# The last stage's norm as a factor per token, and the experts' sums in another place

## The chip, the core and the metric

The kernel runs on one core of one Trainium2 chip. The metric is the time of one execution on the device, in microseconds (us), the median of a few runs. The kernel before took 3516.21 us, median of 3 runs (3515.45 to 3517.61).

## The reference, cut to what matters

The model is two blocks one after the other on 512 tokens of width 1024. What the change touches is the very end: the mixture of experts of the second block, its residual add, and the final norm.

```python
def expert_choice_ffn(h, w_router, w_gate, w_up, w_down):
    ...
    top_aff, top_idx = lax.top_k(jnp.swapaxes(aff, 1, 2), cap)
    xe = jax.vmap(lambda hb, ib: hb[ib])(h, top_idx)
    hid = jax.nn.silu(jnp.einsum('becd,edf->becf', xe, w_gate)) * jnp.einsum('becd,edf->becf', xe, w_up)
    ye = jnp.einsum('becf,efd->becd', hid, w_down) * top_aff[..., None].astype(h.dtype)
    combine = lambda ib, yb: jnp.zeros((L, D), yb.dtype).at[ib.reshape(-1)].add(yb.reshape(-1, D))
    return jax.vmap(combine)(top_idx, ye)
...
        x = x + g2 * expert_choice_ffn(h, w_router[l], w_gate[l], w_up[l], w_down[l])
    return rmsnorm(x, norm_f)
```

There are 16 experts with 64 tokens each. Every expert has a gate, an up and a down matrix of 1024 x 1024 in f32, so the three matrices of all experts are 192 pieces of 1 MB (64 each for `eg`, `eu` and `ed`). The final `rmsnorm` divides each token by the root of its mean square over the 1024 features and multiplies feature by feature with `norm_f`.

## The kernel before

Each stage of the program is a class with one method per engine (`pe`, `act`, `dve`, `pool`, `sp`). The order of the work on an engine is the order in which these methods issue it, stage after stage, written out by hand. Engines meet at semaphores: `P.tick(key)`, `S.tick(key)`, `V.tick(key)` count finished work of TensorE, ScalarE and VectorE, and `e.wait_ge(P.at(key))` waits for it.

The activations stand feature by token: `k.xT[:, c, :]` is chunk c of 8 (128 features x 512 tokens). Two stages matter here.

**Experts.** The experts are taken in 8 pairs (`pr`). For a pair, TensorE runs six wide products (`wide_pe`): m = 0 to 3 are the two halves of the gate and up products, m = 4 and 5 the two halves (512 features each) of the down product. Each is done in two steps `kh`, and each step (16 matmuls of 512 columns) needs two weight pieces of 1 MB. SyncE issues the 24 pieces of a pair into a ring of 11 slots; a slot is loaded again when TensorE has finished the step that read it. In the loop of a pair TensorE does, in this order: m = 0 to 3; the sums of the pair before (`y_pe(pr - 1)`); the transposes of the hidden layer (`hidT`, banks 6 and 7); the gathered tokens of the next pair (`xT_pe`); m = 4 and 5. ScalarE and VectorE then turn banks 4 and 5 into a high and a low part `yhi`, `ylo` (ticks `ye`, one for each half), scaled by the router's weight.

The sums `y` scatter the pair's 128 rows back to the 512 tokens: for each of the 8 chunks c, two matmuls with a one-hot matrix into bank 4 + c % 4, and on VectorE (`y_dve`) one `stt` (line 175) that adds bank times gain into `k.xT[:, c, :]`. For chunk c of 4 or more TensorE waits until VectorE has read chunk c - 4. On VectorE the eight adds stand after the two halves of silu and `hid` (lines 175 and 165) and ahead of the copy of `hidT` (line 2749). The sums of the last pair come after its down product. There VectorE also adds up squares: `stat_act` squares chunk c on ScalarE into one of two buffers, `stat_dve` adds the square into `nacc`, and it stands directly behind the `stt` of the same chunk.

**Output.** One matmul with a matrix of ones adds `nacc` over the partitions and spreads the sum (128 x 512). VectorE makes the mean (line 171) and the reciprocal (line 441), ScalarE the root, all on 128 x 512. VectorE multiplies the eight chunks of x with the norm's weight and this factor (line 175), TensorE turns them back to token by feature with 32 transposes of 128 x 128 (line 282) into six banks, VectorE and ScalarE copy the banks out, and ScalarE issues four DMAs of 128 tokens (512 KB each) to `out_x` (line 2814).

Of the kernel before, what the change touches and what calls it, by code (L numbers as in the profile page):

```python
# [13 lines left out]
D = 1024  # L14
# [2486 lines left out]
class Experts(Dense):  # L2501
# [3 lines left out]
    def __init__(self, k, m):  # L2505
# [22 lines left out]
        self.hid = [piece(4), piece(5)]  # L2528
        self.hidT = [v3(piece(6), 8), v3(piece(7), 8)]
# [3 lines left out]
        self.ends = [(self.V, ("add", 7)), (self.P, ("y", 7, 7))]  # L2533
# [19 lines left out]
    def wide_pe(self, e, pr, m, bank, src):  # L2553

        for kh in range(2):
# [27 lines left out]
    def y_pe(self, e, pr):  # L2583
        k, P, S, V = self.k, self.P, self.S, self.V
        e.wait_ge(V.at(("ye", pr, 1)), V.at(("oh", pr)))
        for c in range(8):
            if c >= 4:
                e.wait_ge(V.at(("y", pr, c - 4)))
            elif c >= 2 and pr < 7:
                e.wait_ge((S if c == 3 else V).at(("xT", pr + 1, c - 2)))  # L2590
            b, cs = k.bank[4 + c % 4], slice(c * 128, c * 128 + 128)
            mm(e, b[:, :], self.yhi[:, cs], self.oh[pr % 2], True, False)
            mm(e, b[:, :], self.ylo[:, cs], self.oh[pr % 2], False, True).then_inc(*P.tick(("y", pr, c)))

    def pe(self, e):
# [18 lines left out]
        for pr in range(8):  # L2614
# [6 lines left out]
            if pr:  # L2621
                self.y_pe(e, pr - 1)
# [10 lines left out]
            for h in range(2):  # L2633
                self.wide_pe(e, pr, 4 + h, B[4 + h], self.hidT[x])
        self.y_pe(e, 7)
# [6 lines left out]
    def act(self, e):  # L2642
# [39 lines left out]
        for c in range(8):  # L2682
            self.stat_act(e, c, k.xT[:, c, :], V.at(("y", 7, c)))
# [10 lines left out]
    def y_dve(self, e, pr):  # L2694
        k = self.k
        for c in range(8):
            e.wait_ge(self.P.at(("y", pr, c)))
            y = k.xT[:, c, :]
            stt(e, y, k.bank[4 + c % 4][:, :], k.MOD[:, 40 + c, 0:1], y, ALU.mult, ALU.add).then_inc(*self.V.tick(("y", pr, c)))
            if pr == 7:  # L2700
                self.stat_dve(e, c, y)

    def dve(self, e):
# [53 lines left out]
        self.y_dve(e, 7)  # L2757
# [18 lines left out]
class Output(Dense):  # L2776


    def __init__(self, k):
        super().__init__(k, "out", "out")  # L2780
        k.reset()
        self.ot = [k.al(1024) for _ in range(4)]
        self.dma = [k.count(f"out_x{i}") for i in range(4)]

# [4 lines left out]

    def pe(self, e):  # L2790
        k, P, S, V, B = self.k, self.P, self.S, self.V, self.k.bank
        self.enter(e)
        self.norm_pe(e, B[7], 512, self.before.V.at(("add", 7)))
        for m in range(8):
            i, k0 = m // 2, 4 * (m % 2)
            if m >= 6:
                e.wait_ge((S if m % 2 else V).at(("ot", m - 6)))
            for c in range(4):
                e.wait_ge(V.at(("scaled", k0 + c)))
                p = k.tr(e, B[m % 6][:, c * 128:c * 128 + 128], k.hT[:, k0 + c, i * 128:i * 128 + 128])  # L2800
            p.then_inc(*P.tick(("ot", m)))
        yield

    def act(self, e):
        k, P, S, V, B = self.k, self.P, self.S, self.V, self.k.bank
        r = k.rstd
        self.enter(e)
        e.wait_ge(V.at("recip"))
        act(e, r, r, ACT.Sqrt).then_inc(*S.tick("rstd"))
        for i in range(4):  # L2810
            e.wait_ge(P.at(("ot", 2 * i + 1)))
            e.h.copy(self.ot[i][:, 512:1024], B[(2 * i + 1) % 6][:, :]).then_inc(*S.tick(("ot", 2 * i + 1)))
            e.wait_ge(V.at(("ot", 2 * i)), S.at(("ot", 2 * i + 1)))
# [3 lines left out]
    def dve(self, e):  # L2817
        k, P, S, V, B = self.k, self.P, self.S, self.V, self.k.bank
        self.enter(e)
        self.norm_dve(e, B[7], 512)  # L2820
        e.wait_ge(S.at("rstd"))
        for c in range(8):
            stt(e, k.hT[:, c, :], k.xT[:, c, :], k.col("normf", c), k.rstd, ALU.mult, ALU.mult).then_inc(
                *V.tick(("scaled", c)))
        for i in range(4):
            e.wait_ge(P.at(("ot", 2 * i)))
            e.h.tensor_copy(self.ot[i][:, 0:512], B[(2 * i) % 6][:, :]).then_inc(*V.tick(("ot", 2 * i)))
# [155 lines left out]
```

## Time and profile before

| what | value |
| --- | --- |
| median of 3 runs | 3516.21 us |
| the profiled execution's own time | 3518.45 us |
| span of its profile | 3516.6 us |
| TensorE busy, share of the span | 3132.0 us, 89% |
| VectorE busy | 1820.3 us, 52% |
| ScalarE busy | 1090.3 us, 31% |
| mean granted TensorE clock | 0.93 of full speed |
| HBM traffic over the whole span | 125 GB/s |

The span runs from the first to the last event of the profile; the execution's own time is 1.85 us longer. Busy times are shares over very different stages. The experts run from about 3001 us to 3494 us of the span, and in most of that the DMA engines move 421 GB/s; from 3469 us on they are idle until the output leaves. The granted clock is either 1.00 (2.4 GHz) or 0.50 (1.2 GHz) in any short stretch, and a mean of both in a longer one.

### The profile page before, as it was taken

How to read it: one execution, taken by the hardware profiler on the slowest of the kernel's cores; microseconds unless marked ns; L12 is line 12 of the kernel's file. 1: busy time of each engine (PE TensorE's matmuls, PEld its weight loads, DVE VectorE, ACT ScalarE, POOL GpSimd, SP SyncE). 2: the span in 40 equal slices, each digit the busy share in tenths (PEclk: the TensorE clock that was granted, in tenths of full speed). 3: DMA queues.
4: the chain of work that ended last, by engine and by line, in shares of the span. 5: the costliest groups of instructions: out<-in, count | busy, mean ns of one | idle time of the engine just before them, and what ended most of it. 6: DMA issues, size and time to landing. Idle time of an engine off the chain costs nothing.

```text
span 3516.6 us, 40774 instructions
## 1 busy us (share of the span) xinstructions
PE 3132.0 (89%) x16694; PEld 2358.2 (67%) x16694; DVE 1820.3 (52%) x3294; ACT 1090.3 (31%) x2156; POOL 41.2 (1%) x75
## 2 busy tenths in 40 slices
PE   7999998879999999999898789999778976788786
PEld 6777667767878878888677678887566974232332
DVE  5444546676656565454566764445763676121213
ACT  3222234353333243332343542222443542000001
POOL 0000000000000000000000000000000100000000
PEclk9999988879999999999898789999788888899998
DMA  4544411102223222221211012222011012899994
GB/s 176 182 168 156 144 48 42 43 25 86 94 72 120 86 94 90 74 77 61 83 48 48 25 60 97 95 96 99 36 60 61 2 62 95 342 421 421 421 421 207
DMA packets 68162, 443.25 MB, mean 126 GB/s; under 512 B 9604, under 2 KB 9732, under 8 KB 21640
## 3 DMA queue, kind: packets, MB, share of 16 engines
q1 hardware_dynamic: 61056, 423.65, 31.7%
q10 hardware_dynamic: 5224, 10.44, 0.8%
q0 software_dynamic: 1696, 6.55, 0.5%
q8 instruction: 132, 2.16, 0.3%
q14 instruction: 54, 0.44, 0.0%
HBM read 435.10 MB, written 5.51 MB: 125 GB/s over the span
## 4 chain that ended last, share of the span: by engine, by line
PE 68%; DVE 17%; DMA 8%; ACT 6%; issue 1%; ACTq 0%; DVEq 0%; POOLq 0%
PE ps L155 66%; DMA b<-in_eu 8%; DVE b L175 7%; DVE b L165 5%; ACT b L181 3%; PE ps L282 1%; DVE b L170 1%; ACT b L382 1%; ACT b L180 1%; DVE b L171 1%; DVE b L721 1%; DVE b L441 1%; ACT L181 0%; DVE b L1813 0%; DMA b<-in_xt 0%
## 5 line engine op out<-in xcount | busy, mean ns | idle before, releaser
L155 PE MATMUL ps<-b,b 128*128 128x512 f32 (+8 forms) x13952 | 2893.2, 399 | 280.9 <-DVE b L165 120.3
L155 PEld LDWEIGHTS ps<-b,b 128*128 128x128 f32 (+4 forms) x13952 | 2159.8, 188 | 986.0 <-issue 342.0
L165 DVE TENSOR_TENSOR b<-b,b 128x1024 fp32r<-128x1024 f32 (+6 forms) x852 | 704.2, 832 | 334.4 <-ACT b L382 230.4
L382 ACT CAST b<-b 128x1024 fp32r<-128x1024 f32 (+2 forms) x408 | 390.9, 960 | 441.0 <-PE ps L155 436.0
L165 DVE TENSOR_TENSOR b<-ps,b 128x64 f32<-128x64 f32 (+4 forms) x601 | 207.7, 356 | 260.8 <-PE ps L155 223.9
L181 ACT ACTIVATE b<-b 128x512 f32<-128x512 f32 (+6 forms) x303 | 170.5, 567 | 316.6 <-DVE b L175 163.4
L175 DVE SCALAR_TENSOR_TENSOR b<-ps,b 128x512 f32<-128x512 f32 (+3 forms) x296 | 150.5, 529 | 217.0 <-PE ps L155 190.1
L165 DVE TENSOR_TENSOR b<-b,ps 128x512 f32<-128x512 f32 (+1 forms) x106 | 71.8, 678 | 291.6 <-PE ps L155 291.1
L175 DVE SCALAR_TENSOR_TENSOR b<-b,b,b 128x512 f32<-128x512 f32 (+4 forms) x292 | 181.1, 641 | 68.4 <-ACT b L181 62.9
L155 PE MATMUL ps<-b 64*64 64x64 f32 (+8 forms) x2272 | 190.1, 278 | 16.4 <-DVE b L1994 9.2
L155 PEld LDWEIGHTS ps<-b 64*64 64x64 f32 (+3 forms) x2272 | 146.2, 150 | 52.1 <-issue 25.9
L1379 ACT CAST b<-b 128x512 fp32r<-128x512 f32 x88 | 54.6, 620 | 399.8 <-DVE b L165 399.8
L282 PE MATMUL ps<-b,b 128*128 128x128 f32 (+2 forms) x470 | 84.3, 320 | 83.4 <-DVE b L175 32.7
L175 DVE SCALAR_TENSOR_TENSOR b<-ps,b,b 128x512 f32<-128x512 f32 (+2 forms) x144 | 80.6, 589 | 130.5 <-ACT b L181 112.4
L282 PEld LDWEIGHTS ps<-b,b 128*128 128x128 f32 (+2 forms) x470 | 62.0, 163 | 116.1 <-DVE b L175 42.0
L181 ACT ACTIVATE b<-b,b 128x128 f32<-128x128 f32 (+1 forms) x224 | 90.5, 444 | 127.9 <-DVE b L165 113.5
L181 ACT ACTIVATE b<-ps 128x256 f32<-128x256 f32 (+5 forms) x78 | 27.6, 367 | 272.3 <-PE ps L155 271.1
L181 ACT ACT_TABLE_LOAD x70 | 89.8, 1283 | 30.9 <-DVE b L441 21.0
L175 DVE SCALAR_TENSOR_TENSOR b<-b,b 128x512 f32<-128x512 f32 (+5 forms) x142 | 86.7, 612 | 16.1 <-ACT b L181 14.8
L175 DVE SCALAR_TENSOR_TENSOR b<-b,ps 128x512 f32<-128x512 f32 x16 | 11.0, 687 | 142.8 <-ACT b L181 142.8
L181 ACT ACTIVATE b<-ps,b 128x128 f32<-128x128 f32 (+2 forms) x136 | 51.9, 419 | 103.8 <-PE ps L155 103.8
L951 ACT COPY b<-ps 128x128 f32<-128x128 f32 x240 | 61.4, 266 | 71.7 <-PE ps L155 60.2
(98 smaller groups left out, 659.8 us busy)
## 6 DMA issues: line engine op xcount, KB each, us to landing
b<-in_eg SPq DMA_DIRECT2D x64, 1024.0 KB, 21.0
b<-in_eu SPq DMA_DIRECT2D x64, 1024.0 KB, 19.5
b<-in_ed SPq DMA_DIRECT2D x64, 1024.0 KB, 21.7
b<-in_wg SPq DMA_DIRECT2D x44, 1024.0 KB, 4.8
b<-in_wu SPq DMA_DIRECT2D x44, 1024.0 KB, 4.8
b<-in_win SPq DMA_DIRECT2D x40, 1024.0 KB, 4.8
b<-in_wd SPq DMA_DIRECT2D x48, 768.0 KB, 4.3
b<-in_wmod SPq DMA_DIRECT2D x24, 1024.0 KB, 4.9
```

Source lines behind the costliest of these rows:

```text
L155: return e.h.matmul(out, l, r, start=start, stop=stop)
L165: return e.h.tensor_tensor(out, a, b, op)
L170: return e.h.tensor_scalar(out, a, s1, None, op0)
L171: return e.h.tensor_scalar(out, a, s1, s2, op0, op1)
L175: return e.h.scalar_tensor_tensor(out, a, s, b, op0, op1)
L180: return e.h.activation(out, a, f, bias=bias, scale=scale, accum_out=acc)
L181: return e.h.activation(out, a, f, bias=bias, scale=scale)
L282: return e.h.transpose(out, i, self.K["ident"][0:n, 0:n])
L382: e.h.copy(hi, src).then_inc(*self.S.tick(("hi", i)))
L441: e.h.reciprocal(r, r).then_inc(*self.V.tick("recip"))
L951: e.h.copy(self.LB[q][:, 0:128], B[:, 0:128]).then_inc(*S.tick((s, j, "L", lev + 1)))
L1379: e.h.copy(self.ahi[:, f - self.f0[grp], :], t).then_inc(*S.tick(("ahi", f)))
```

## The change

Three things are changed, in the experts' stage and in the output's.

1. In pairs 1 to 7 the sums of the pair before (`y_pe(pr - 1)`) are issued on TensorE behind m = 0 instead of behind m = 3, and on VectorE the eight adds come ahead of silu.
2. The last pair's sums are done in two halves. Chunks 0 to 3, which need only m = 4, go between the two steps `kh` of m = 5, chunks 4 to 7 behind the second. They use all eight banks. The add of a chunk's square is put behind the `stt` of the next chunk. ScalarE writes, behind each square, the chunk times the norm's weight into a new tile `fin`.
3. The output turns `fin`, not the normed chunks. The sum of squares comes out per token as four matmuls with one column (`ms`, 128 x 4: a partition is a token), so that mean, reciprocal and root are done on 128 x 4, and the factor is applied in the copy out of the banks, as a scale per partition. A root of a dummy value (`warm`) stands on ScalarE ahead of the wait for the reciprocal.

```diff
-        self.ends = [(self.V, ("add", 7)), (self.P, ("y", 7, 7))]
+        self.ends = [(self.V, ("y", 7, 7)), (self.P, ("y", 7, 7)), (self.S, ("ye", 7, 1))]
...
-            if pr:
-                self.y_pe(e, pr - 1)
+                if pr and m == 0:
+                    self.y_pe(e, pr - 1)
...
-            for h in range(2):
-                self.wide_pe(e, pr, 4 + h, B[4 + h], self.hidT[x])
-        self.y_pe(e, 7)
+            self.wide_pe(e, pr, 4, B[4], self.hidT[x])
+            if pr < 7:
+                self.wide_pe(e, pr, 5, B[5], self.hidT[x])
+        self.wide_pe(e, 7, 5, B[5], self.hidT[1], (0,))
+        self.y_pe(e, 7, range(4))
+        self.wide_pe(e, 7, 5, B[5], self.hidT[1], (1,))
+        self.y_pe(e, 7, range(4, 8))
...
-        for c in range(8):
-            self.stat_act(e, c, k.xT[:, c, :], V.at(("y", 7, c)))
+                for c in range(4 * h, 4 * h + 4) if pr == 7 else ():
+                    x_ = k.xT[:, c, :]
+                    self.stat_act(e, c, x_, V.at(("y", 7, c)))
+                    act(e, self.fin[:, c, :], x_, ACT.Copy, scale=k.col("normf", c)).then_inc(*S.tick(("fin", c)))
...
-            if pr == 7:
-                self.stat_dve(e, c, y)
+            if pr == 7 and c % 4:
+                self.stat_dve(e, c - 1, k.xT[:, c - 1, :])
+        if pr == 7:
+            self.stat_dve(e, cs[-1], k.xT[:, cs[-1], :])
...
+            if pr:
+                self.y_dve(e, pr - 1)
             for h in range(2):
                 e.wait_ge(S.at(("tanh", pr, h)))
...
-            if pr:
-                self.y_dve(e, pr - 1)
             e.wait_ge(P.at(("hidT", pr, 0)))
...
     def pe(self, e):
...
-        self.norm_pe(e, B[7], 512, self.before.V.at(("add", 7)))
...
+        for i, h in self.order:
+            if (i, h) == (3, 1):
+                b = k.bank[7]
+                e.wait_ge(x.V.at(("add", 7)))
+                for t in range(4):
+                    p = mm(e, b[:, t:t + 1], k.nacc[:, t * 128:t * 128 + 128], k.K["one"][:, 0:1])
+                p.then_inc(*P.tick("sum"))
+                e.wait_ge(V.at("mean"))
             for c in range(4):
...
+                e.wait_ge(x.S.at(("fin", 4 * h + c)))
+                p = k.tr(e, self.bank(i, h)[:, c * 128:c * 128 + 128], x.fin[:, 4 * h + c, i * 128:i * 128 + 128])
...
     def act(self, e):
...
+        act(e, self.warm, k.K["one"][:, 0:1], ACT.Sqrt)
         e.wait_ge(V.at("recip"))
-        act(e, r, r, ACT.Sqrt).then_inc(*S.tick("rstd"))
+        act(e, self.ms, self.ms, ACT.Sqrt).then_inc(*S.tick("rstd"))
+        e.wait_ge(S.at("rstd"))
         for i in range(4):
...
+            act(e, self.ot[i][:, 0:512], self.bank(i, 0)[:, :], ACT.Copy, scale=self.ms[:, i:i + 1]).then_inc(*S.tick(("ot", i)))
```

The transposes come in the order (token block i, feature half h) = (0,0), (1,0), (2,0), (3,0), (0,1), (1,1), (2,1), (3,1), four transposes each into bank 4h + i.

On VectorE, the last pair's turn in the experts' stage reads before as follows (lines 175 and 165 with b_323 and b_324 are silu and `hid` of the two halves, b_62 is `k.xT`, the copy into b_317 is `hidT`):

```order
L175 SCALAR_TENSOR_TENSOR b_323<-b_323,ps 128x512
L165 TENSOR_TENSOR b_317<-b_323,ps 128x512
L175 SCALAR_TENSOR_TENSOR b_324<-b_324,ps 128x512
L165 TENSOR_TENSOR b_317<-b_324,ps 128x512
L175 SCALAR_TENSOR_TENSOR b_62<-ps,b_67,b_62 128x512 x8
L2749 COPY b_317<-ps 128x512
```

In the changed kernel the same rows stand in this order:

```order
L175 SCALAR_TENSOR_TENSOR b_62<-ps,b_67,b_62 128x512 x8
L175 SCALAR_TENSOR_TENSOR b_323<-b_323,ps 128x512
L165 TENSOR_TENSOR b_317<-b_323,ps 128x512
L175 SCALAR_TENSOR_TENSOR b_324<-b_324,ps 128x512
L165 TENSOR_TENSOR b_317<-b_324,ps 128x512
L2765 COPY b_317<-ps 128x512
```

The eight adds of the pair before have moved from between `hid` and the copy to the front.

On ScalarE the end of the program is, in the changed kernel, from the second half of the last pair's `yhi` (b_330) on (b_71 and b_72 are the squares, b_316 holds `fin`, b_340 is `ms`, b_341 is `warm`):

```order
L181 ACTIVATE b_330<-ps,b_326 128x512
L181 ACTIVATE b_71<-b_62 128x512
L181 ACTIVATE b_316<-b_62,b_56 128x512
L181 ACTIVATE b_72<-b_62 128x512
L181 ACTIVATE b_316<-b_62,b_56 128x512
...
L181 ACT_TABLE_LOAD
L181 ACTIVATE b_341<-b_54 128x1
L181 ACTIVATE b_340<-b_340 128x4
L181 ACTIVATE b_336<-ps,b_340 128x512
L2840 DMA out_x<-b_336 128x1024
```

Every square has a second activation behind it, the same group of four squares and four `fin` also stands ahead of the first row, and the load of the table stands behind the last `fin` and ahead of the small root.

On TensorE the end of the changed program is this (b_335 is the one-hot matrix, b_330 and b_331 are `yhi` and `ylo`, b_64 is `nacc`):

```order
L155 MATMUL ps<-b_335,b_330 128x512
L155 MATMUL ps<-b_335,b_331 128x512
L282 MATMUL ps<-b_54,b_316 128x128 x28
L155 MATMUL ps<-b_54,b_64 128x1 x4
L282 MATMUL ps<-b_54,b_316 128x128 x4
```

Before, it was these three kinds of rows, with the sum over the squares ahead of all transposes:

```order
L155 MATMUL ps<-b_335,b_330 128x512
L155 MATMUL ps<-b_335,b_331 128x512
L155 MATMUL ps<-b_64,b_54 128x512
L282 MATMUL ps<-b_54,b_63 128x128 x32
```

28 of the 32 transposes now stand ahead of the sum, and they read `fin` where they read the normed chunks.

## Rows read from the trace of the kernel before

**Rows 1.** Timeline of TensorE in the last pair (start us, us, what, idle before):
```profile
3439.67 3.65 PE L155 MATMUL ps<-b,b 128*64 128x512 f32 x16 [1.31 <-DMA b<-in_eg]
3444.64 3.65 PE L155 MATMUL ps<-b,b 128*64 128x512 f32 x16 [1.32 <-DMA b<-in_eu]
```
**Rows 2.** Windows (PE, PEld, DVE, ACT, POOL busy; PEclk; DMA share, GB/s):
```profile
3469.00:3469.50 0.50, 0.50 (x6) 0.24 (x4) 0.00 (x0) 0.00 (x0) 0.00 (x0) 1.00 0.00 0
```
**Rows 3.** The chain that ended last, to the down product (start us, us):
```profile
3449.61 3.67 PE ps L155 x16
3453.37 0.69 DVE b L165
3454.06 4.62 DVE b L175 x7
3458.72 0.67 PE ps L282 x4
...
3460.76 15.66 PE ps L155 x64
3476.45 0.70 ACT b L181
```
**Rows 4.** The chain, the last pair's sums:
```profile
3477.97 0.74 PE ps L155 x2
3478.74 1.42 DVE b L175 x2
...
3480.85 0.69 DVE b L165
3481.54 0.67 DVE b L175
```
**Rows 5.** The chain, the output stage:
```profile
3493.89 2.09 PE ps L155 x2
...
3496.79 3.36 DVE b L441
...
3500.25 1.28 ACT L181
...
3502.20 5.40 DVE b L175 x8
3507.65 5.10 PE ps L282 x25
3512.77 0.58 ACT b L2812
```
**Rows 6.** Timeline: the last output DMA's issue on ScalarE's queue:
```profile
3513.44 0.34 ACTq L2814 DMA_DIRECT2D out_x<-b  x1
```
**Rows 7.** Timeline: TensorE from one pair's down product into the next pair:
```profile
3401.66 17.39 PE L155 MATMUL ps<-b,b 128*64 128x512 f32 x80
```
**Rows 8.** Timeline of ScalarE: a copy of `hidT`, two squares in a row:
```profile
3460.08 0.58 ACT L2672 COPY b<-ps 128x512 f32<-128x512 f32 x1 [16.12 <-PE ps L282]
...
3479.52 1.29 ACT L181 ACTIVATE b<-b 128x512 f32<-128x512 f32 x2 [2.39 <-DVE b L175]
```
**Rows 9.** The chain: eight transposes at the full clock:
```profile
3400.61 1.11 PE ps L282 x8
```
**Rows 10.** Windows, the granted clock at the end (columns as in Rows 2):
```profile
3461.00:3461.50 0.50, 0.50 (x2) 0.00 (x0) 0.00 (x0) 0.00 (x0) 0.00 (x0) 0.50 0.99 410
3484.00:3485.00 1.00, 0.70 (x2) 0.30 (x2) 0.30 (x2) 0.63 (x1) 0.00 (x0) 0.88 0.00 0
3512.00:3513.00 1.00, 0.73 (x6) 0.50 (x4) 0.66 (x1) 0.39 (x2) 0.00 (x0) 0.96 0.67 274
```
**Rows 11.** Groups by shape, whole span (busy us, mean ns, idle before):
```profile
L155 PE MATMUL ps<-b,b 128*128 128x4 f32 x88 | 13.5, 288 | 7.7 <-DVE b L170 7.7
L2022 DVE RECIPROCAL b<-b 128x4 f32<-128x4 f32 x8 | 1.4, 178 | 0.3
L170 DVE TENSOR_SCALAR b<-ps,b 128x512 f32<-128x512 f32 x4 | 3.0, 751 | 19.4 <-PE ps L155 19.4
```

More of the change, by code:

```diff
@@ L2528, in __init__ @@
         self.hid = [piece(4), piece(5)]
+        self.fin = v3(hh, 8)
         self.hidT = [v3(piece(6), 8), v3(piece(7), 8)]
@@ L2551, in sp, with wide_pe @@
         yield
-    def wide_pe(self, e, pr, m, bank, src):
-        for kh in range(2):
+    def wide_pe(self, e, pr, m, bank, src, halves=(0, 1)):
+        for kh in halves:
             n = 24 * pr + 4 * m + 2 * kh
@@ L2581, in xT_pe, with ybank, y_pe @@
             self.tr_pe(e, "xT", pr, h, self.xe[pr % 2])
-    def y_pe(self, e, pr):
-        k, P, S, V = self.k, self.P, self.S, self.V
-        e.wait_ge(V.at(("ye", pr, 1)), V.at(("oh", pr)))
-        for c in range(8):
-            if c >= 4:
+    def ybank(self, pr, c):
+        return self.k.bank[c if pr == 7 else 4 + c % 4]
+    def y_pe(self, e, pr, cs=range(8)):
+        P, S, V = self.P, self.S, self.V
+        for c in cs:
+            e.wait_ge(V.at(("ye", pr, c // 4 if pr == 7 else 1)), V.at(("oh", pr)))
+            if pr == 7:
+                e.wait_ge(V.at(("hid", 7, c // 2)) if c < 4 else S.at(("ye", 7, c - 4)) if c < 6 else
+                          (S if c == 7 else V).at(("hidT", 7, c - 6)))
+            elif c >= 4:
                 e.wait_ge(V.at(("y", pr, c - 4)))
-            elif c >= 2 and pr < 7:
+            elif c >= 2:
                 e.wait_ge((S if c == 3 else V).at(("xT", pr + 1, c - 2)))
-            b, cs = k.bank[4 + c % 4], slice(c * 128, c * 128 + 128)
-            mm(e, b[:, :], self.yhi[:, cs], self.oh[pr % 2], True, False)
-            mm(e, b[:, :], self.ylo[:, cs], self.oh[pr % 2], False, True).then_inc(*P.tick(("y", pr, c)))
+            b, f = self.ybank(pr, c), slice(c * 128, c * 128 + 128)
+            mm(e, b[:, :], self.yhi[:, f], self.oh[pr % 2], True, False)
+            mm(e, b[:, :], self.ylo[:, f], self.oh[pr % 2], False, True).then_inc(*P.tick(("y", pr, c)))
     def pe(self, e):
@@ L2681, in act @@
                     *S.tick(("ye", pr, h)))
-        for c in range(8):
-            self.stat_act(e, c, k.xT[:, c, :], V.at(("y", 7, c)))
+                for c in range(4 * h, 4 * h + 4) if pr == 7 else ():
+                    x_ = k.xT[:, c, :]
+                    self.stat_act(e, c, x_, V.at(("y", 7, c)))
+                    act(e, self.fin[:, c, :], x_, ACT.Copy, scale=k.col("normf", c)).then_inc(*S.tick(("fin", c)))
         yield
@@ L2692, in xT_dve, with y_dve @@
         e.h.tensor_copy(self.xeT[pr % 2][:, 0:4, :], v3(self.k.bank[6][:, :], 4)).then_inc(*V.tick(("xT", pr, 0)))
-    def y_dve(self, e, pr):
+    def y_dve(self, e, pr, cs=range(8)):
         k = self.k
-        for c in range(8):
+        for c in cs:
             e.wait_ge(self.P.at(("y", pr, c)))
             y = k.xT[:, c, :]
-            stt(e, y, k.bank[4 + c % 4][:, :], k.MOD[:, 40 + c, 0:1], y, ALU.mult, ALU.add).then_inc(*self.V.tick(("y", pr, c)))
-            if pr == 7:
-                self.stat_dve(e, c, y)
+            stt(e, y, self.ybank(pr, c)[:, :], k.MOD[:, 40 + c, 0:1], y, ALU.mult, ALU.add).then_inc(*self.V.tick(("y", pr, c)))
+            if pr == 7 and c % 4:
+                self.stat_dve(e, c - 1, k.xT[:, c - 1, :])
+        if pr == 7:
+            self.stat_dve(e, cs[-1], k.xT[:, cs[-1], :])
     def dve(self, e):
@@ L2756, in dve @@
                     ALU.subtract).then_inc(*V.tick(("ye", pr, h)))
-        self.y_dve(e, 7)
+                if pr == 7:
+                    self.y_dve(e, 7, range(4 * h, 4 * h + 4))
         yield
@@ L2782, in __init__ @@
         self.ot = [k.al(1024) for _ in range(4)]
+        self.ms, self.warm = k.al(8)[:, 0:4], k.al(8)[:, 0:1]
         self.dma = [k.count(f"out_x{i}") for i in range(4)]
+        self.order = [(i, h) for h in range(2) for i in range(4)]
     def sp(self, e):
@@ L2817, in dve @@
     def dve(self, e):
-        k, P, S, V, B = self.k, self.P, self.S, self.V, self.k.bank
+        k, P, S, V = self.k, self.P, self.S, self.V
         self.enter(e)
-        self.norm_dve(e, B[7], 512)
+        e.wait_ge(P.at("sum"))
+        ts(e, self.ms, k.bank[7][:, 0:4], 1.0 / D, ALU.mult, EPS, ALU.add).then_inc(*V.tick("mean"))
+        e.wait_ge(V.at("mean"))
+        e.h.reciprocal(self.ms, self.ms).then_inc(*V.tick("recip"))
         e.wait_ge(S.at("rstd"))
-        for c in range(8):
-            stt(e, k.hT[:, c, :], k.xT[:, c, :], k.col("normf", c), k.rstd, ALU.mult, ALU.mult).then_inc(
-                *V.tick(("scaled", c)))
         for i in range(4):
-            e.wait_ge(P.at(("ot", 2 * i)))
-            e.h.tensor_copy(self.ot[i][:, 0:512], B[(2 * i) % 6][:, :]).then_inc(*V.tick(("ot", 2 * i)))
+            e.wait_ge(P.at(("turn", i, 1)))
+            ts(e, self.ot[i][:, 512:1024], self.bank(i, 1)[:, :], self.ms[:, i:i + 1], ALU.mult).then_inc(*V.tick(("ot", i)))
         yield
```

20 lines of the change are left out of this document (7 added, 13 removed).

## The prediction

> **What bounds the kernel now.** I read the windows of the experts' stage first, then the chain of waits, then the timeline of the last 80 us. In the stretch of the pairs the DMA engines are the limit: each wide step takes TensorE 3.65 us and starts 4.97 us after the one before, with 1.31 us of waiting for a weight piece between them [rows 1]. So the last pieces arrive when the DMA queue gets to them, and TensorE's order changes nothing there as long as slots are given back in time; the DMA engines fall idle at 3469.0 [rows 2]. What can be moved is what comes after the last weights. The chain shows it in three parts: from the last up product to the start of the down product, 3453.37 to 3460.76, with 4.62 us of the other pair's adds in it [rows 3]; from the down product's end at 3476.45 through the last sums to the squares' sum at 3493.89 [rows 3 to 5]; and the output stage up to the last DMA issue at 3513.44 [rows 6], which is 3.16 us ahead of the end of the span, 3516.6.
>
> **Sums behind m = 0.** In the last pair the path from `hid` to the down product loses the 4.62 us of adds. What is left: `hid` done at 3454.06, the second group of four transposes 0.67 [rows 3], ScalarE's copy 0.58 [rows 8], and about 0.15 of hand-overs: the down product can start at 3455.5, 5.3 us earlier. But now it meets the weights. Continuing the 4.97 us rhythm [rows 1] from the step at 3449.61 [rows 3], its four steps have their pieces at 3454.6, 3459.6, 3464.5 and 3469.0 to 3469.5 [rows 1 to 3]. So steps one to three run 3455.5, 3459.6 and 3464.5, and the third ends its issue at 3468.1. The 64 matmuls that took 15.66 us in one run, the first of them at clock 0.50 [rows 3, 10], no longer matter as a block.
>
> The moved work itself is eight chunks, VectorE bound: `stt` every 0.66 us (4.62 for 7), of which TensorE stands through about 4 us, since it needs only chunk 3's add for chunk 7. Behind m = 0 this makes the next step late by about 2.9 us (4 us less the 1.3 us of waiting), and each of the next steps wins back 1.4 us when it runs without waiting. After three it is on the rhythm again, ahead of m = 3. Before, the delay was longer: TensorE came back to the weights late enough for 80 matmuls in one piece of 17.39 us [rows 7]. I cost this edit at nothing in pairs 1 to 6. Its cover is the ring; if the cover failed, every pair would pay up to 2.9 us.
>
> **The last sums in two halves.** Chunks 0 to 3 go on TensorE at 3468.1 for 8 matmuls, at 0.21 us each (0.43 per pair, as in a wide step) 1.75 us. The last step then starts at 3469.9, not at 3469.4, and its product is ready for ScalarE 3.7 us later at 3473.6; before this was 3476.45 [rows 3]. Now a new wait: ScalarE has squares and `fin` of chunks 0 to 3 ahead of it. Two activations in a row take 1.29 us [rows 8], so four chunks take 4 x 1.29 = 5.2 us, from 0.77 us behind VectorE's first `stt` at 3468.9: ScalarE is free at 3474.85. That holds back `yhi` by 1.25 us, and behind it `ylo`, TensorE and VectorE. With 1.5 us for `yhi` and `ylo` (3476.45 to 3477.97) and 0.77 to the first `stt` [rows 3, 4], the first `stt` of the second half is at t0 = 3477.1, where the old first `stt` was at 3478.74. Part one gives 1.6 us.
>
> Then four chunks instead of eight. Before, a chunk costs 2.05 us, because `stt`, square and add go round in a ring: add 0.69, `stt` 0.67, square 0.64 and gaps [rows 4]. After, the add waits for the next `stt`, and ScalarE with two activations per chunk sets the pace at 1.29 us. From t0: first square at 0.77, the fourth at 0.77 + 3 x 1.29 = 4.64, its end 5.28, the last add seen by TensorE at 6.05, the last `fin` at 5.93. Before, from TensorE's first sum at 3477.97 to the sum over squares at 3493.89: 15.92 [rows 4, 5]. After: 0.77 + 6.05 = 6.8. Part two gives 9.1 us.
>
> **The output stage.** Before, from 3493.89 to the last issue at 3513.44: 19.55 us, in it the 2.09 us matmuls, 3.36 reciprocal, 1.28 table load, 5.40 for eight `stt` and 5.10 for the last 25 transposes [rows 5, 6]. After, TensorE may start turning when the last `stt` is done (the stage's entry wait), t0 + 4.1, for `fin` of chunks 0 to 3 has been there long. The price of a transpose is 0.139 us at the full clock (8 in 1.11) [rows 9] and about 0.2 at the half clock (25 in 5.10) [rows 5]. I take the half clock: before, the clock fell at about 3484.9 [rows 10], some 4 us after TensorE's last dense work, and here TensorE is nearly idle from 3473.6 to t0 + 4.1 = 3481.2 but for 1.75 us. So 28 transposes run to t0 + 9.5, and the wait for the last `fin` (5.93) and for the last add (6.05) is covered by them. The four one-column matmuls have no row; the nearest is 288 ns for four columns, with overlap 0.8 us for all four, bounded by 0.4 and 1.2 [rows 11]. The sum is there at 10.4. Mean and reciprocal on 128 x 4 are 0.18 each [rows 11], the small root some 0.2, each with a hand-over: the factor is ready at t0 + 11.3, while the last four transposes finish at 11.9 beside it. The table load that ends 1.28 us behind the last `fin`, at 7.2, is off the path.
>
> The copies out are 0.69 to 0.75 us on each engine [rows 11]. ScalarE also issues the DMAs: 0.69 + 0.34 for the issue [rows 6] + 0.14 of waits = 1.17 us per block. First issue t0 + 12.05, last t0 + 15.55. So 9.5 us from the last add to the last issue, 10.05 less than 19.55. From the last issue to the end I keep 3.16 us; the four blocks together (2.1 MB at 421 GB/s, 5.0 us, started about 0.9 us behind the first issue) end at t0 + 18 and ask for no more.
>
> Sum: 1.6 + 9.1 + 10.05 = 20.8 us. The end of the span is 3477.1 + 15.55 + 3.16 = 3495.8 against 3516.6; the execution's own time would be 3518.45 - 20.8 = 3497.7. That execution was 2.2 us above the median of the runs, so the median becomes 3516.2 - 20.8 = **3495.4 us**.
>
> The skill and the trace part on one thing here. Row first: with almost only transposes on TensorE from 3507.65 the clock went back to 1.00 near 3512 [rows 5, 10]. The Trainium skill (TensorE: Matmul & The Clock Gate, Part 4: PE-mode transpose) says that the full clock does not engage for transpose-mode work, since it does not count as busy in the same way. By that rule all 32 transposes run at the half clock and the sum stands at 3495.4; by the row they may bring the clock back about 4.5 us after they start, which takes some 0.5 us off. The row, not the rule, leaves the next rival its chance.
>
> **Rivals.**
> - *The clock stays full in the tail (12%).* For it: at 3478 to 3484 it stayed at 1.00 with short gaps [rows 10]. Against it: 7.6 us nearly idle. 28 transposes in 3.9 us instead of 5.4, and 0.4 us less on the sums and the last group: 1.9 us less, 3493.5.
> - *The two engines do not overlap as drawn (22%).* Each chunk of the second half then pays part of the old ring again: 2.05 instead of 1.29 us, 0.76 x 4 = 3.0 us, and in the first half the same 3.0 us hold `yhi` back, of which I count half, since only one of two engines would have to be late: 3495.4 + 3.0 + 1.5 = 3499.9. The hand-overs in the trace are short (0.02 to 0.05 us between the pieces of the chain), which speaks against it.
> - *The ring gives slots back too late (3%).* Each of 7 pairs pays the 2.9 us: 20.3 us, and the gain is gone, 3515.7. Against it: in the old order TensorE was later than that in each pair and the rhythm stayed 4.97 us.
> - *TensorE loses its clock in the pairs (2%), the case on the slow side.* The adds now cut the stretch behind m = 0, and TensorE has gaps at every step. If the half clock is granted there, a step takes twice its 3.4 us back to back, 6.85 us, against 4.97 us of DMA: 12 steps x 1.9 = 23 us per pair, about 3600 over four pairs or more. It decides as soon as two pairs are hit. Against it: the steps with 1.31 us gaps ran at the full rate [rows 1]; the one drop in the pairs' stretch, at 3461, came after the sums and transposes with no wide product for 7 us [rows 3, 10], a pattern that the change takes away.
>
> **How the numbers follow.** Forecast 61%, the rivals as given. The forecast's own spread is 3494 to 3498 (the one-column matmuls, copies and issue, and run to run scatter of 1 us either side). The range reaches to both near rivals: 3491.5 to 3500.5. About 0.2% of this time, 7 us, is what a measurement can tell from no change. Faster by more: 0.95 (forecast, first two rivals); within it 0.03; slower 0.02.
>
> **What would show it.** In the changed profile: the last step of the down product starts near 3469.9 and not before 3469; ScalarE goes from the `fin` of chunk 3 straight to `yhi` near 3474.8; the add rows at the end are 1.3 us apart, not 2.05; 28 transposes take 4 us (clock 1.00) or 5.4 us (0.50); the reciprocal is 0.18 us; the last output DMA is issued near 3492.7. It is wrong if the wide steps of pairs 1 to 7 leave the 4.97 us rhythm, if DMA share falls below 1.0 there, or if TensorE waits for ScalarE's `fin` in the second group of transposes.

## The result and the profile after

| | kernel before | changed kernel |
| --- | --- | --- |
| median (runs) | 3516.91 us (4) | 3491.0 us (4), 3484.16 to 3495.92 |
| profiled execution, own time | 3518.45 us | 3490.62 us |
| span of its profile | 3516.6 us | 3488.8 us |

The ratio is 0.993, with a 95% interval of 0.9918 to 0.9941, so whole runs are 21 to 29 us shorter; how much of that is the change's own is worked out below. The forecast was 3495.4 us, 20.8 us off, with a range of 3491.5 to 3500.5; the median lies 0.5 us below that range.

The span became 27.8 us shorter, but not all of it by the change. The experts' stage begins with TensorE's first wide matmul, at 3001.64 us before and at 2995.61 us now, and the program ahead of that point is the same in both. So 6.0 us of the 27.8 were gone before the first changed instruction, and 21.8 us lie behind it. Here is the chain of the changed kernel (start us, us, what; pieces called `issue`, none above 0.14 us, are left out), the counterpart of [rows 3 to 5]:

```profile
3433.63 3.67 PE ps L155 x16
3437.32 21.04 DMA b<-in_ed
3458.49 4.34 PE ps L155 x18
3462.86 0.76 DVE b L175
3463.64 5.22 ACT b L181 x9
3468.88 0.76 DVE b L175
3469.69 0.75 PE ps L155 x2
3470.46 0.76 DVE b L175
...
3473.86 0.67 DVE b L175
3474.58 4.94 PE ps L282 x28
3479.52 0.80 PE ps L155 x8
3480.34 0.17 DVE b L171
3480.54 0.19 DVE b L2849
3480.75 0.21 ACT b L181
3480.99 0.75 DVE b L170
```

The adds between the last up step and the down product [rows 3] are gone, and in their place stands a DMA: the chain comes to the down product from the landing of `in_ed`. Then ScalarE has nine activations in a row (5.22 us), which are the squares and `fin` of chunks 0 to 3 and after them `yhi` of the second half. The reciprocal of 3.36 us [rows 5] takes 0.19 us, and the sum over the squares (line 155, x8) stands behind 28 transposes. These are the four one-column matmuls: the profile has two rows for each, as it has two for the one matmul of the old sum [rows 5].

The timeline of TensorE in the last pair shows where it waits now (start us, us, idle before in brackets), to be held against [rows 1 and 3]:

```profile
3438.62 3.65 PE L155 MATMUL ps<-b,b 128*64 128x512 f32 x16 [1.33 <-DMA b<-in_eu]
3443.59 3.65 PE L155 MATMUL ps<-b,b 128*64 128x512 f32 x16 [1.32 <-DMA b<-in_eu]
...
3449.47 3.65 PE L155 MATMUL ps<-b,b 128*64 128x512 f32 x16 [0.72 <-issue]
3453.52 3.65 PE L155 MATMUL ps<-b,b 128*64 128x512 f32 x16 [0.39 <-DMA b<-in_ed]
...
3458.49 9.30 PE L155 MATMUL ps<-b,b 128*64 128x512 f32 x40 [1.32 <-DMA b<-in_ed]
```

The rhythm of 4.97 us is the old one up to the last up step at 3443.59. The down product starts 5.9 us after that, where it took 11.15 us before, and then it waits for its weights twice. The third step, the eight matmuls of chunks 0 to 3 and the fourth step run as one piece of 9.30 us.

Since the program ahead of the experts' stage varies by itself, I measure all runs below from one mark, the start of the last pair's last up step (16 matmuls), to the end of the span. From here on "the mark" is that start. The stretch is 3516.6 - 3449.61 = **66.99 us** before and 3488.8 - 3443.59 = **45.21 us** now: 21.78 us less.

### The profile page after: what moved, and what is told of

Read it like the earlier page. It is cut to its first block, busy times and chain, and to the rows that moved or that the text cites. A ratio compares the mean times of both kernels' runs of the same rounds, so it can differ in the third digit from the quotient of the medians.

```text
span 3488.8 us, 40788 instructions
## 1 busy us (share of the span) xinstructions
PE 3121.4 (89%) x16700; PEld 2351.5 (67%) x16700; DVE 1809.8 (52%) x3286; ACT 1094.7 (31%) x2165; POOL 41.2 (1%) x75
## 4 chain that ended last, share of the span: by engine, by line
PE 68%; DVE 15%; DMA 9%; ACT 6%; issue 1%; ACTq 0%; DVEq 0%; POOLq 0%
PE ps L155 67%; DVE b L175 5%; DVE b L165 5%; DMA b<-in_eg 5%; DMA b<-in_eu 3%; ACT b L181 3%; PE ps L282 1%; DVE b L170 1%; ACT b L382 1%; ACT b L180 1%; DVE b L171 1%; DVE b L721 1%; DMA b<-in_ed 1%; DVE b L441 0%; ACT L181 0%
## 5 line engine op out<-in xcount | busy, mean ns | idle before, releaser
L181 ACT ACTIVATE b<-b,b 128x128 f32<-128x128 f32 (+2 forms) x232 | 96.2, 454 | 128.3 <-DVE b L165 113.9
L181 ACT ACTIVATE b<-ps,b 128x128 f32<-128x128 f32 (+3 forms) x140 | 54.7, 428 | 122.3 <-PE ps L155 120.8
L180 ACT ACTIVATE b<-b,b 128x128 f32<-128x128 f32 (+3 forms) x64 | 35.4, 554 | 136.7 <-DVE b L170 136.7
```

The lines of the kernel that those rows point to most:

```text
L180: return e.h.activation(out, a, f, bias=bias, scale=scale, accum_out=acc)
L181: return e.h.activation(out, a, f, bias=bias, scale=scale)
```

## The experiments

**The moved sums alone.** The kernel before with the first part of the change:

```diff
-            if pr:
-                self.y_pe(e, pr - 1)
+                if pr and m == 0:
+                    self.y_pe(e, pr - 1)
```

and `y_dve(e, pr - 1)` ahead of silu.

> The kernel before with the first part alone: in pairs 1 to 7 the sums of the pair before stand behind m = 0. I measure from TensorE's first wide matmul of the experts' stage to the end of the span; that was 514.96 us before and 493.19 us in the changed kernel. Theory (the last weights decide): the down product's steps run at the pace at which their pieces land, so it ends 3.4 us earlier, not 5.3, and all that follows is as before: 511.6 us. Rival (the adds' 4.6 to 5.3 us come off whole): 509.7 to 510.3. Rival (the moved sums make TensorE late and the gain is given back): 514 to 515, and the steps of m = 0 to 3 leave the 4.97 us rhythm. The part of the program ahead of the stage should vary by several us from run to run without any relation to this edit.

Measured: 3515.2 - 3002.94 = 512.26 us from the first wide matmul, 63.75 us from the mark, 3.24 less than before. Whole runs: ratio 0.9998 (0.9984 to 1.0012), since the scatter of whole runs hides 3 us. Its timeline at the down product:

```profile
3451.45 3.65 PE L155 MATMUL ps<-b,b 128*64 128x512 f32 x16 [1.31 <-DMA b<-in_eu]
...
3457.34 3.65 PE L155 MATMUL ps<-b,b 128*64 128x512 f32 x16 [0.72 <-issue]
3461.37 3.65 PE L155 MATMUL ps<-b,b 128*64 128x512 f32 x16 [0.38 <-DMA b<-in_ed]
...
3466.35 3.65 PE L155 MATMUL ps<-b,b 128*64 128x512 f32 x16 [1.33 <-DMA b<-in_ed]
3471.29 3.65 PE L155 MATMUL ps<-b,b 128*64 128x512 f32 x16 [1.28 <-DMA b<-in_ed]
3474.99 0.69 ACT L181 ACTIVATE b<-ps,b 128x512 fp32r<-128x512 f32 x1 [9.24 <-PE ps L155]
```

Three of four steps wait for a piece of `in_ed`. The start came 5.3 us earlier (5.89 us behind the mark instead of 11.15), the end only 3.3 us (23.54 instead of 26.84 for ScalarE's second `yhi`). The weights decide, as the first theory has it; the adds do not come off whole. How large these 3.3 us are also depends on the clock that the old order gets at this place, which the repeats at the end of this section show.

**The later add alone.** The kernel before with this edit:

```diff
-            if pr == 7:
-                self.stat_dve(e, c, y)
+            if pr == 7 and c:
+                self.stat_dve(e, c - 1, k.xT[:, c - 1, :])
+        if pr == 7:
+            self.stat_dve(e, 7, k.xT[:, 7, :])
```

> The kernel before with one edit: in the last pair's sums the add of a chunk's square stands behind the stt of the next chunk. I measure from the last up step of the last pair (the start of its 16 matmuls) to the end of the span, where everything is tied to the weights' arrival: 66.99 us before, 45.21 in the changed kernel. Theory (the ring of stt, square and add is opened, and VectorE sets the pace at 1.27 to 1.36 us per chunk instead of 2.05): 61.4 to 62.0, a gain of 5.0 to 5.6. Rival (ScalarE's two buffers of squares or the banks close another ring, 1.7 us and more per chunk): 64 or more.

Measured: 3518.4 - 3456.93 = 61.47 us from the mark, 5.52 less (whole runs 0.9988, 0.9967 to 1.0009). VectorE and ScalarE in its sums:

```profile
3490.04 0.74 DVE L175 SCALAR_TENSOR_TENSOR b<-ps,b,b 128x512 f32<-128x512 f32 x1
3490.70 0.68 DVE L165 TENSOR_TENSOR b<-b,b 128x512 f32<-128x512 f32 x1
3490.82 0.63 ACT L181 ACTIVATE b<-b 128x512 f32<-128x512 f32 x1 [0.63 <-DVE b L175]
3491.30 0.74 DVE L175 SCALAR_TENSOR_TENSOR b<-ps,b,b 128x512 f32<-128x512 f32 x1
```

VectorE goes from `stt` to add to `stt` without a wait, 1.26 us per chunk; it was 2.05 us [rows 4], since the add waited 0.70 us for the square of the same chunk. From ScalarE's second `yhi` to the end of the last add it takes 12.19 us instead of 17.38, 5.19 less. The other 0.33 us are in the output stage, whose last 25 transposes took 4.34 us in this profile and 5.08 before.

**The output stage alone.** The kernel before with the changed output stage, and with `fin` written by ScalarE behind each square (`act(e, self.fin[:, c, :], x_, ACT.Copy, scale=k.col("normf", c))`, as in the change); the last sums as before.

> The kernel before with the third part alone (the output turns x times the norm's weight, the factor comes in per token, fin is written by ScalarE behind each square; the last sums stay in one piece, each add directly behind its own stt). From the stage's first wide matmul to the end, 514.96 us before. Theory: the last add of squares ends as before (fin hides in ScalarE's 1.4 us of idling per chunk), the 28 transposes start one stt after the last, and the first output DMA is issued about 7.2 us behind the last stt of the sums, the last 3.5 us later, the end 3.5 us after that: 505.2 to 505.7, a gain of 9.5. Rival (fin slows the ring of stt, square and add by 0.7 us per chunk): 511. Rival (the table load for the root is on the path): 507.

Measured: 3506.5 - 2999.89 = 506.61 us from the first wide matmul and 58.73 us from the mark, 8.26 less (whole runs 0.9974, 0.9957 to 0.9991). That is about 1 us short of what I expected, and by its number alone the run lies nearer to the rival of the table load (507) than to the theory (505.2 to 505.7). The rows decide. One part of what is missing is in the 28 transposes:

```profile
3491.14 5.96 PE L282 MATMUL ps<-b,b 128*128 128x128 f32 x28 [7.04 <-DVE b L175]
```

They took 5.96 us here, where the changed kernel needs 4.94 for the same 28. Here TensorE had idled 7.04 us ahead of them, and its granted clock was 0.50 until about 3496.7. The other part is `fin`. The pace of the later chunks was 2.05 us in spite of it (`stt` at 3484.19 and 3486.24 of its timeline), but the first two chunks come close together, and there the first `fin` stands between two squares. These are the second chunk's add before and in this run:

```profile
3480.85 0.69 DVE L165 TENSOR_TENSOR b<-b,b 128x512 f32<-128x512 f32 x1 [0.70 <-ACT b L181]
```

```profile
3479.49 0.69 DVE L165 TENSOR_TENSOR b<-b,b 128x512 f32<-128x512 f32 x1 [1.17 <-ACT b L181]
```

So `fin` cost the ring 0.47 us once, and not 0.7 us per chunk. The table load, 3492.38 to 3493.66, was over long before the root at 3498.41. Both rivals fall.

**The halves undone.** The changed kernel with all of `y_pe(7)` behind the down product, ScalarE's squares and `fin` behind both `yhi`, VectorE's eight `stt` in one run:

```diff
         self.wide_pe(e, 7, 5, B[5], self.hidT[1], (0,))
+        self.wide_pe(e, 7, 5, B[5], self.hidT[1], (1,))
         self.y_pe(e, 7, range(4))
-        self.wide_pe(e, 7, 5, B[5], self.hidT[1], (1,))
         self.y_pe(e, 7, range(4, 8))
```

> The changed kernel with the last pair's sums in one piece behind the whole down product; all eight banks, the later add and the output stage as in the changed kernel. From the stage's first wide matmul to the end, 493.19 us in the changed kernel. Theory: four more chunks at ScalarE's pace of 1.14 us stand behind the last weights, less the 1.2 us by which the first half had held the last step and yhi back: 496.6. Rival (the halves cost as much as they bring, since TensorE's last step waits for the first half's matmuls and ScalarE's queue): 493.2. Rival (each chunk costs the old 2.05 us): 500 or more.

Measured: 3481.9 - 2986.98 = 494.92 us from the first wide matmul. That number is misleading, since the first pair's 128 matmuls ran 29.09 us here and 30.27 us in the changed kernel, at another granted clock. From the mark it is 3481.9 - 3433.81 = 48.09 us against 45.21: the halves bring 2.88 us. ScalarE's second `yhi` starts 1.05 us earlier without them (23.54 instead of 24.59 us behind the mark), and from there to the end of the last add it takes 3.93 us more (11.75 instead of 7.82). I had expected 3.4; the pace is 1.26 us per chunk here, too, where the rival had 2.05.

**Turning earlier.** The changed kernel with another order in the output stage on TensorE:

```diff
-        self.enter(e)
         for i, h in self.order:
-            if (i, h) == (3, 1):
+            if h == 0:
+                e.wait_ge(x.V.at(("y", 7, i)))
+            if (i, h) == (0, 1):
+                self.enter(e)
                 b = k.bank[7]
...
                 p.then_inc(*P.tick("sum"))
+            if (i, h) == (3, 1):
                 e.wait_ge(V.at("mean"))
```

> The changed kernel with another order in the output stage on TensorE: the 16 transposes of features 0 to 511 wait only for their own bank's stt and stand in the idle stretch ahead of the last sums' end, then come the four one-column matmuls, then the other 16 transposes. From the stage's first wide matmul to the end, 493.19 us in the changed kernel. Theory (the factor waits for the 28 transposes ahead of the sum): the factor is ready at the end of the last add plus 1.7 us, the first DMA 3.3 us earlier, the end 3.3 us earlier: 489.9. Rival (the four output DMAs and their bandwidth set the end, not the factor): the first DMA is earlier, but the end is less than 1.5 us earlier: 492 or more. Rival (the last transposes follow the sum and are now what the copies wait for): 491.5.

Measured: 3500.6 - 3458.51 = 42.09 us from the mark, 3.12 less than the changed kernel. From the first wide matmul it is 488.90 us, 1 us under the expected 489.9; there, too, the first pair was quicker (29.02 us against 30.27). The start of its stage, though, was at 3011.70, 16 us later than in the changed kernel's profile, so its whole time there was longer. The rows of the tail:

```profile
3487.51 2.57 PE L282 MATMUL ps<-b,b 128*128 128x128 f32 x16
...
3490.23 0.69 DVE L165 TENSOR_TENSOR b<-b,b 128x512 f32<-128x512 f32 x1 [0.19 <-ACT b L181]
...
3491.07 1.02 PE L155 MATMUL ps<-b,b 128*128 128x1 f32 x8 [0.99 <-DVE b L165]
3491.95 1.94 PE L282 MATMUL ps<-b,b 128*128 128x128 f32 x16
...
3493.56 0.36 ACTq L2843 DMA_DIRECT2D out_x<-b  x1
```

The first 16 transposes now stand in the idle stretch, and the sum starts right behind the last add. So in the changed kernel the factor waited for the 28 transposes ahead of it, and the DMAs' bandwidth did not yet cover that.

**The same with ScalarE in another order.** In addition `fin` of chunks 0 to 3 behind the second `yhi`, and the dummy root ahead of the last pair's `hidT` copy:

```diff
+            if pr == 7:
+                act(e, self.warm, k.K["one"][:, 0:1], ACT.Sqrt)
...
+                if pr == 7 and h:
+                    for c in range(4):
+                        self.fin_act(e, c)
                 for c in range(4 * h, 4 * h + 4) if pr == 7 else ():
-                    x_ = k.xT[:, c, :]
-                    self.stat_act(e, c, x_, V.at(("y", 7, c)))
-                    act(e, self.fin[:, c, :], x_, ACT.Copy, scale=k.col("normf", c)).then_inc(*S.tick(("fin", c)))
+                    self.stat_act(e, c, k.xT[:, c, :], V.at(("y", 7, c)))
+                    if h:
+                        self.fin_act(e, c)
```

> The run with the early turn (e4_turn_early), and ScalarE's work in another order: fin of chunks 0 to 3 behind the second half's yhi, in ScalarE's idle time, and the dummy root that brings the table stands ahead of the last pair's hidT copy. From the last up step to the end, 42.09 us in that run, 45.21 in the changed kernel. Theory (fin of the first half holds yhi back by 0.35 us; the table load is hidden either way): 41.6 to 41.8. Rival (the hold by ScalarE is as large as the prediction had it, 1.25 us): 40.9. Rival (the square and copy functions are not there in the root's table, so that it is loaded again): 43 or more. As a whole program it should be 25 to 30 us faster than the kernel before.

Measured: 3491.0 - 3449.13 = 41.87 us from the mark, 0.22 less than the run before it and 0.07 outside what I had written. `yhi` now starts behind TensorE's last step and no longer behind `fin`, and the table was not loaded again. `t0`, the first `stt` of the second half, came 0.32 us earlier, but the last 16 transposes took 2.97 us instead of 1.94, with the clock at 0.50 from 3483 on. Whole runs: 3494.32 us, median of 6, ratio to the kernel before 0.994 (0.992 to 0.9959); the run with the early turn alone had 3490.86 us, median of 4, 0.992 (0.9903 to 0.9936). Both beat the kernel before. Neither can be told from the changed kernel by whole runs; that they beat it rests on the 3.1 and 3.3 us in the traced tail.

**Both kernels once more.**

> The changed kernel once more, without an edit, to see how much of the 26 us between the medians belongs to it. From the last up step to the end 45.2 us again, within 0.3. The experts' stage begins at 2995.6 us in the changed kernel's first profile and at 3001.6 in that of the kernel before, although the program ahead of it is the same. Theory (chance: the granted clock in the two mixers falls differently in every execution): the start of the stage lies anywhere from 2985 to 3012 us, and the median of whole runs goes back to 3517 less 21.8, so 3494 to 3497. Rival (the edit somehow makes the early stages faster): the start is near 2995 again and the median 3490 to 3492.

> The kernel before once more, without an edit. From the last up step to the end 67.0 us again, within 0.3. Theory (chance in the early stages): the start of the experts' stage differs from 3001.6 us by several us and the ratio of times is 1.000, with an interval that is wider than 0.001. Rival (the kernel before is steady and its start is always near 3001): the start lies within 1 us of it.

Measured: the changed kernel 3491.87 us, median of 6 (3487.36 to 3496.56), ratio 0.9931 (0.9915 to 0.9946); from the mark 3488.7 - 3443.69 = 45.01 us. The kernel before 3513.06 us, median of 12 (3502.27 to 3523.74), ratio to its other runs 0.9998 (0.9983 to 1.0013); from the mark 3504.8 - 3439.26 = 65.54 us. The last is 1.45 less than 66.99 and outside what I expected. One row has the cause, the down product of the kernel before in the second profile:

```profile
3450.42 13.95 PE L155 MATMUL ps<-b,b 128*64 128x512 f32 x64 [0.72 <-DVE b L2749]
```

It took 15.66 us in the first profile [rows 3], with the clock at 0.50 for its beginning [rows 10]; here the windows around it show 1.00:

```profile
3449.00:3450.00 1.00, 0.69 (x5) 0.42 (x4) 0.69 (x1) 0.27 (x1) 0.00 (x0) 1.00 0.96 401
3450.00:3451.00 1.00, 0.58 (x4) 0.35 (x6) 0.00 (x0) 0.32 (x1) 0.00 (x0) 1.00 1.02 426
3451.00:3452.00 1.00, 1.00 (x8) 0.39 (x6) 0.00 (x0) 0.00 (x0) 0.00 (x0) 1.00 1.02 426
```

The other two profiles with the old order, the output stage alone and the later add alone, had 15.65 us. So the old order loses the clock at this place in three of four profiles, and the new order in none of six. Why one execution of the old order kept it is not shown. It does change what the moved sums are worth: ScalarE's second `yhi` stood 26.84 us behind the mark in the first profile, 25.15 in the second and 23.54 with the sums moved, so they bring 3.3 us where the old order loses its clock and 1.6 us where it does not. The whole change brings 65.54 - 45.01 = 20.53 us by the two repeats, against 21.78 by the first two profiles.

The start of the experts' stage, with the same program ahead of it, was at 3001.64 and 2992.49 us (before), 2995.61 and 2996.95 (changed), and in the other runs at 2986.98, 2999.89, 3002.34, 3002.94, 3008.91 and 3011.70. The two profiles of the kernel before alone are 9.15 us apart, so a difference of 6.0 us needs no edit. The spread over all ten is 24.7 us, and its two ends were measured on one and the same chip. The mixers are a place where it shows. These windows are of the halves undone (start at 2986.98) and of the early turn (3011.70), each the stretches 440 to 840 and 1700 to 2080 us; the last three columns are the granted clock, the DMA share and GB/s:

```profile
440.00:840.00 400.00, 340.31 (x1737) 279.90 (x1738) 246.46 (x486) 166.79 (x369) 0.00 (x0) 0.86 0.12 43
1700.00:2080.00 380.00, 326.14 (x1712) 271.10 (x1710) 234.25 (x468) 157.65 (x357) 0.00 (x0) 0.88 0.12 45
```

```profile
440.00:840.00 400.00, 342.83 (x1705) 279.95 (x1706) 242.39 (x481) 164.87 (x366) 0.00 (x0) 0.83 0.12 43
1700.00:2080.00 380.00, 328.04 (x1642) 268.85 (x1642) 227.89 (x461) 153.80 (x351) 0.00 (x0) 0.82 0.12 42
```

The quicker execution had the higher clock in both and got further: 1712 matmuls against 1642 in the second stretch. Why the clock differs from one execution to the next is open. The repeat of the changed kernel, with its start at 2996.95 and its median of 3491.87, fell on the numbers of the rival (near 2995, 3490 to 3492) and not on those of the theory (3494 to 3497). Two things speak against the rival all the same. In the second profile of the kernel before the stage started at 2992.49, earlier than in either of the changed kernel's. And I had taken the median from 3517: in the 23 runs of the kernel before that belong to these last four measurements it was 3513.84, and 3513.84 - 21.8 = 3492.0. In the 19 that belong to the first four it had been 3517.01. So that the edit makes the early stages faster is not borne out, but two profiles of each kernel do not exclude a small part of it.

## Why the prediction was right

The forecast was 20.8 us, and behind the mark it was 21.78 by the first two profiles and 20.53 by the repeats. By its steps (t0 is the first `stt` of the second half):

| step | forecast | measured |
| --- | --- | --- |
| down product's start behind the mark | 5.9 us | 5.88 us |
| first `stt` of the first half behind the mark | 19.3 | 19.27 |
| ScalarE free for the second `yhi` | 25.2 | 24.59 |
| t0 behind the mark | 27.5 | 26.87 |
| last add seen by TensorE, from t0 | 6.05 | about 5.6 |
| 28 transposes | 5.4 | 4.94 |
| factor ready, from t0 | 11.3 | 10.53 |
| first and last output DMA, from t0 | 12.05, 15.55 | 11.31, 14.84 |
| last issue to the end | 3.16 | 3.5 |

**What bounded it.** The mechanism is the one that the prediction gave: the down product starts 5.3 us earlier and is then held by its weights. The moved sums alone show it by themselves, with 3.24 us instead of 5.3. In pairs 1 to 6 nothing changed, as it was costed: the 4.97 us rhythm and 421 GB/s stayed, and from the stage's first wide matmul to the mark it is 447.97 us before and 447.98 us now.

**The hold by ScalarE** was there, but smaller. The prediction put two activations at 1.29 us; the rows show 1.13 to 1.14 us from one square to the next with a `fin` between them, although their own durations are 0.61 to 0.63 and 0.71:

```profile
3464.79 0.61 ACT L181 ACTIVATE b<-b 128x512 f32<-128x512 f32 x1
3465.31 0.71 ACT L181 ACTIVATE b<-b,b 128x512 f32<-128x512 f32 x1
...
3465.92 0.61 ACT L181 ACTIVATE b<-b 128x512 f32<-128x512 f32 x1
```

The overlap makes the hold 0.35 to 0.4 us instead of 1.25; taking `fin` out of the way brought t0 from 26.87 to 26.55 us behind the mark. In the second half the two engines are nearly level. VectorE needs 1.26 us for `stt` and add and so sets when the last `stt` is done and the transposes start, 4.12 us behind t0 (forecast 4.1). ScalarE runs its four squares and four `fin` without a gap, and the last add still waits for its square:

```profile
3475.31 0.69 DVE L165 TENSOR_TENSOR b<-b,b 128x512 f32<-128x512 f32 x1 [0.19 <-ACT b L181]
```

So ScalarE sets the end of the adds, as forecast, at 1.14 us per chunk instead of 1.29, and the transposes cover it. ScalarE was free for `yhi` 0.6 us earlier than forecast, because the 1.29 us of [rows 8] are the span of one pair of activations, which the prediction took as the distance from pair to pair.

**The transposes and the clock.** The prediction took the half clock for all 28. The windows of the changed kernel show it for about two thirds of their 4.94 us:

```profile
3474.50:3475.36 0.86, 0.78 (x7) 0.79 (x8) 0.67 (x3) 0.86 (x3) 0.00 (x0) 0.95 0.00 0
3475.36:3478.70 3.34, 3.34 (x18) 3.34 (x16) 0.64 (x1) 2.01 (x3) 0.00 (x0) 0.50 0.00 0
3478.70:3480.00 1.30, 1.30 (x14) 1.30 (x13) 0.00 (x0) 0.00 (x0) 0.00 (x0) 1.00 0.00 0
```

The clock fell at about 3475.3 and came back at about 3478.7, 4.1 us after the transposes began, while TensorE did nothing but transposes since 3474.58. So the rule of the Trainium skill that the prediction weighed (TensorE: Matmul & The Clock Gate, Part 4: PE-mode transpose) does not hold for these transposes; the row of before was the better guide. The rival of a clock that stays full did not come true either: 4.94 us lies between its 3.9 and the 5.4. It is what the prediction gave as the row's alternative, some 0.5 us less than the half clock throughout. How soon the clock comes back varies: with transposes alone on TensorE it took from 3.1 us (the changed kernel's repeat) to about 5.5 us (the output stage alone).

**The output's end.** The last output DMA was issued 14.84 us behind t0, and the end came 3.5 us after it, not 3.16. The four transfers now follow each other without a gap, and the DMA share is 0.97 to 1.02 in every window from 3483 to 3487:

```profile
3482.00:3483.00 1.00, 0.00 (x0) 0.00 (x0) 1.00 (x3) 0.69 (x1) 0.00 (x0) 0.55 0.39 160
3483.00:3484.00 1.00, 0.00 (x0) 0.00 (x0) 0.72 (x2) 0.63 (x1) 0.00 (x0) 0.50 0.97 393
...
3486.00:3487.00 1.00, 0.00 (x0) 0.00 (x0) 0.00 (x0) 0.00 (x0) 0.00 (x0) 0.50 1.00 401
3487.00:3488.00 1.00, 0.00 (x0) 0.00 (x0) 0.00 (x0) 0.00 (x0) 0.00 (x0) 0.50 0.82 324
```

So what matters there is the first issue, and a quicker issue on ScalarE's queue would bring next to nothing. That last point is read from the trace and was not tried.

**The parts together.** Alone, the moved sums bring 3.24, the later add 5.52 and the output stage 8.26 us; the halves bring 2.88 in the presence of the rest. That is 19.90 of 21.78. Split at two points that every profile has, the rest can be placed (us; the profile of the kernel before is the first one):

| stretch | before | moved sums | later add | output stage | without halves | changed |
| --- | --- | --- | --- | --- | --- | --- |
| mark to ScalarE's second `yhi` | 26.84 | 23.54 | 26.84 | 26.84 | 23.54 | 24.59 |
| from there to the last add's end | 17.38 | 17.38 | 12.19 | 17.86 | 11.75 | 7.82 |
| from there to the end | 22.77 | 22.83 | 22.44 | 14.03 | 12.80 | 12.80 |

The three parts alone add up to 17.02, and the kernel that has all three without the halves is 18.90 us quicker than the kernel before. Of the 1.88 us between, 0.92 lies in the sums: 0.44 between the later add alone (12.19) and the run without halves (11.75), where the sums of chunks 0 to 3 have banks of their own and need not wait for the second half's `ylo`, and 0.48 is what `fin` costs the old ring (17.86 against 17.38) and not the opened one, whose pace is 1.26 us with it and without it. The other 0.96 lies in the output stage, mostly in the 28 transposes, 5.96 us in the output stage alone and 4.89 with the halves undone.

**The level.** What the prediction did not see is the scatter of the start of the stage. It had three runs within 2.2 us and took 1 us either side; in 12 later runs the kernel before spread over 21 us. The forecast of 3495.4 is 4.4 us from the median of 3491.0. Of that, 1.0 is the sum. The other 3.4 are that level. With them the median lies 0.5 us below the stated range of 3491.5 to 3500.5 and below the forecast's own spread of 3494 to 3498; the repeat's 3491.87 lies just inside the range. By the medians alone even the rival of the full clock (3493.5) was nearer than the forecast, and only the traced tail tells the two apart. As for the level, the profile after has 6.0 us from ahead of the change, and the kernel before has its middle at 3517.01 in one set of 19 runs and at 3513.84 in another of 23.

**The rivals.** Engines that do not overlap: refuted by the pace of 1.26 us and less per chunk. Slots given back too late, and the clock lost in the pairs: refuted by the rhythm and by a granted clock of 1.00 from 3100 to 3400 us.

## What to carry to other kernels

When weights stream in at the DMA limit, only the work behind the last landing can be shortened: count from that landing, and an earlier start upstream turns into waiting (5.3 us earlier gave 3.3 us here, and 1.6 where the old order kept its clock). Where early stages vary by chance, weigh parts of 3 us from a mark in the trace that lies ahead of the edit. A reduction on two engines in which each step waits for the other's answer to the same chunk is opened by working one chunk behind (2.05 to 1.26 us per chunk here). A factor that is the same for a whole row belongs behind the work that does not need it, on the smallest tile that holds it (reciprocal 3.36 to 0.19 us), and what stands ahead of it in an engine's queue should be work that is ready earlier (3.1 us here).

## What the runs showed of the hardware

- Executions of one program differ by more than the three first runs showed: the start of the last stages was 9.15 us apart in two profiles of the kernel before and varied by 24.7 us over ten profiles with the same instructions ahead of it, and between the two ends of that range the mean granted clock differed by 0.03 and 0.06 in the two mixers.
- Transposes alone on TensorE brought the granted clock from 0.50 back to 1.00. The plainest case is the output stage alone, where TensorE had idled for 7.04 us and the clock was 1.00 about 5.5 us after the first transpose; in the changed kernel it took 4.1 us, in its repeat 3.1.
- The same order of work, with the same gaps, lost the clock in three profiles and kept it in one (64 matmuls in 15.65 to 15.66 us or in 13.95).
- On ScalarE a square and a scaled copy of 128 x 512, issued in turn without a gap, take 1.13 to 1.14 us from one square to the next, though the two durations add up to 1.32 us.
- A load of the activation table behind the last tanh held for squares, scaled copies and the root: in the last variant there was no second load.
